# Two-layer diffusion trunk on one core: residual with tokens on partitions, down and output projections with weight rows moving

## The chip, the core and the metric

The kernel runs on one core of a Trainium2 chip. TensorE (PE in the profile) multiplies, VectorE (DVE), ScalarE (ACT) and GpSimd (POOL) work on SBUF, the on-chip memory with 128 partitions, and SyncE (SP) issues the transfers from HBM. A matmul holds a stationary operand of 128x128, whose load is a record of its own (PEld), and streams a moving operand of up to 512 columns through it into one of eight accumulator banks of 128 partitions by 512 floats (PSUM). The metric is the device time of one execution in microseconds (us), as the median of several runs; smaller is better.

## The reference, cut to what matters

There are two layers over 256 context and 256 latent tokens (one sequence of 512 here) of 1024 features. The mixing itself (attention, neighbourhood attention, delta rule, state space) does not change. What the change touches are the norms around each stage and the products before them:

```python
def rms_norm(x, g):
    xf = x.astype(jnp.float32)
    y = xf * lax.rsqrt(jnp.mean(xf * xf, axis=-1, keepdims=True) + RMS_EPS)
    return (y * g.astype(jnp.float32)).astype(x.dtype)

def modulate(x, g_pre, shift, scale):
    return rms_norm(x, g_pre) * (1.0 + scale) + shift

def half_ffn(v, shift, scale, gate, g_pre, g_post, w1, w3, w2):
    out = swiglu(modulate(v, g_pre, shift, scale), w1, w3, w2)   # (silu(h @ w1) * (h @ w3)) @ w2
    return v + 0.5 * gate * rms_norm(out, g_post)

# one layer, for the latent tokens h (the context hc has the same weights and its own modulation)
    h = half_ffn(h, ml[0], ml[1], ml[2], g[0], g[1], ffn1_w1[l], ffn1_w3[l], ffn1_w2[l])
    ul = modulate(h, g[2], ml[3], ml[4])
    y_lat, y_ctx = token_mixing(ul, uc, ...)                     # ends in [a, b, c, d] @ w_out
    h = h + ml[5] * rms_norm(y_lat, g[3])
    h = half_ffn(h, ml[6], ml[7], ml[8], g[4], g[5], ffn2_w1[l], ffn2_w3[l], ffn2_w2[l])
```

So a norm over the features of each token stands before and after each of three stages per layer. w1 and w3 are 1024x2816, w2 is 2816x1024, w_out is 1024x1024. In the last layer the context is not needed after the mixing, so its last FFN runs on 256 latent tokens. The nine modulation vectors of a layer come from `silu(c) @ w_mod`.

## The kernel before

**Arithmetic.** Each factor is kept as a high part, rounded to fp32r, and a low part, the rest. A product is three matmuls (`split_product`, lines 885 to 887): high by high, high by low, low by high.

**Layout.** Residual and activations have features on partitions: `xT` is 8 blocks of 128 features by 512 tokens. In every product of an FFN and of the output projection a 128x128 block of weights is stationary and 512 tokens move. One FFN has two parts. Each part has 11 "up" pieces (a block of w1 and of w3, 8 feature blocks each, 48 matmuls of 512 columns) into banks 0 to 3, a silu on ACT, a product on DVE and a split into `hh` and `hl`, and then 8 "down" pieces (1408 floats per partition, 33 matmuls of 512 columns), each of which gives one block of 128 output features in bank 4 or 7. The part's results are collected in `uT` by DVE. The last FFN already has weights moving in its down projection: `hh_last` and `hl_last` are stationary there, and `x_turn` (L1478) and `gate_rows` (L1487) bring residual and gain to that layout; its tail from L2066 on ACT and L2818 on DVE norms and adds token tiles of 128.

**Weights.** SP brings pieces of 2048 floats per partition (512 KB) into a ring of four slots, ACT rounds a piece to `wh` (L1617), DVE subtracts to get `wl` (`split_rest`, L2137) or, for the first piece of a stage, POOL does (`split_first`, L2874). `wh` and `wl` have two buffers (`wh_in`, `wl_in` for the input projection), so piece n waits for the products of piece n-2.

**Gaps.** Between two stages (five times: after the first FFN and after the output projection of each layer, and after the second FFN of layer 0) nothing can be multiplied until the norm of the result, the residual and the norm of the new residual are done. Before, with features on partitions, the sum over features goes through TensorE: DVE squares and adds blocks (`y_block`, L2240, L2243), PE adds over partitions (`token_sums`, L841), ACT takes the root (L1622), DVE the reciprocal (L2189), and PE broadcasts it (`spread`, L833). Then DVE scales (L2254) and adds (L2258, blocks 2 and 5 on POOL), ACT squares (L1657), and the same way leads through sums, root and spread to DVE L2218 and L2214, to the high parts on ACT and the low parts on DVE (L2230, L2225) and POOL. PE has three modulation products in each of these gaps (`mod_product`, L818; `GAP_MODS = 3`), which it does while it waits, with a small turn (L798) behind them. The first piece of the next stage then goes through feature blocks k = 0 to 7 as they come.

**Order.** All five engines have instruction streams written out by hand, which meet by semaphores. Within an engine nothing overtakes.

## Time and profile before

| | us |
|---|---|
| median of 3 runs | 2214.09 (2212.1 to 2214.68) |
| profiled execution | 2218.34 |
| its span, first to last instruction | 2216.5 |
| mean granted TensorE clock | 0.966 |

| engine | busy us | share of the span | instructions |
|---|---|---|---|
| PE | 2080.9 | 94% | 12805 |
| DVE | 1060.7 | 48% | 1570 |
| ACT | 788.0 | 36% | 1201 |
| POOL | 199.6 | 9% | 298 |

Busy time says how full an engine is over the whole. The chain that ended last says whose work sets the end at each moment. For this kernel the windows between two stages have to be read by themselves, since the average hides them: the stage before ends with its last product, and the next one runs evenly again with its second piece. Of HBM the transfers take 116 GB/s on average.

### The profile page before, as it was taken

To read this page: it belongs to the slowest core of one execution; us is meant where nothing else is said; L and a number is where in the kernel's file an instruction comes from. 1 tells how busy PE (TensorE), PEld (TensorE's weight loads), DVE (VectorE), ACT (ScalarE), POOL (GpSimd) and SP (SyncE) were. 2 spreads that over 40 slices of the span, in tenths; PEclk is the share of its full clock that TensorE was granted. 3 is DMA by queue.
4 is the path that set the end of the run, shared out by engine and by line. 5 is a ranking of instruction groups with operands and counts; after the bars stand their busy time and mean duration, and the time that the engine had idled before them with its cause. 6 is when DMAs were issued, how large, how long until landed. Compare 5 with 4: busy or idle time off the path is not lost.

```text
span 2216.5 us, 30333 instructions
## 1 busy us (share of the span) xinstructions
PE 2080.9 (94%) x12805; PEld 1700.1 (77%) x12805; DVE 1060.7 (48%) x1570; ACT 788.0 (36%) x1201; POOL 199.6 (9%) x298
## 2 busy tenths in 40 slices
PE   6999999899989998999999899999979987888998
PEld 4778888687846776888888688888859764687997
DVE  5233333566285576333334633333464548475554
ACT  3222222354335335221223522222344434344443
POOL 0000000100024421000000100000010022521000
PEclk8999999999999999999999899999988998899999
DMA  9554443423236433424423432432342311335653
GB/s 293 162 172 130 125 110 85 148 77 100 69 115 217 153 96 96 114 66 117 113 72 106 119 97 76 121 95 73 112 131 69 107 39 39 115 115 153 181 185 109
DMA packets 383752, 258.88 MB, mean 117 GB/s; under 512 B 21738, under 2 KB 379392, under 8 KB 383616
## 3 DMA queue, kind: packets, MB, share of 16 engines
q1 hardware_dynamic: 383616, 256.94, 39.5%
q8 instruction: 101, 1.65, 0.3%
q14 instruction: 35, 0.29, 0.0%
HBM read 255.86 MB, written 1.05 MB: 116 GB/s over the span
## 4 chain that ended last, share of the span: by engine, by line
PE 81%; DVE 12%; ACT 3%; issue 1%; SPq 1%; POOL 1%; DMA 0%; DVEq 0%; ACTq 0%; POOLq 0%
PE bank L885 23%; PE bank L886 23%; PE bank L887 23%; PE bank L818 2%; PE bank L1252 1%; DVE mlaw L2480 1%; DVE arena L2487 1%; DVE uT L2254 1%; PE bank L1390 1%; DVE small L2508 1%; DVE wl L2137 1%; PE bank L841 1%; PE bank L833 1%; ACT wh L1617 1%; PE bank L1361 1%
## 5 line engine op out<-in xcount | busy, mean ns | idle before, releaser
L885 PE MATMUL bank<-uh,wh 128*128 128x512 f32 (+1 forms) x1504 | 548.7, 365 | 11.1 <-DVE ul L2230 6.5
L887 PE MATMUL bank<-uh,wl 128*128 128x512 f32 (+1 forms) x1504 | 545.8, 363 | 0.0
L886 PE MATMUL bank<-ul,wh 128*128 128x512 f32 (+1 forms) x1504 | 545.8, 363 | 0.0
L2137 DVE TENSOR_TENSOR wl<-ring,wh 128x2048 fp32r<-128x2048 f32 (+1 forms) x150 | 311.7, 2078 | 175.6 <-ACT wh L1617 175.4
L1617 ACT ACTIVATE wh<-ring 128x2048 fp32r<-128x2048 f32 (+1 forms) x153 | 266.3, 1741 | 304.9 <-PE bank L887 293.0
L885 PEld LDWEIGHTS bank<-uh,wh 128*128 128x128 f32 x1504 | 286.1, 190 | 61.7 <-issue 12.0
L887 PEld LDWEIGHTS bank<-uh,wl 128*128 128x128 f32 x1504 | 285.9, 190 | 43.7
L886 PEld LDWEIGHTS bank<-ul,wh 128*128 128x128 f32 x1504 | 286.1, 190 | 43.0
L2276 DVE TENSOR_TENSOR arena<-arena,bank 128x512 f32<-128x512 f32 x66 | 45.4, 688 | 353.0 <-PE bank L887 353.0
L885 PE MATMUL bank<-hh,wh 128*128 128x512 f32 x528 | 205.5, 389 | 0.0
L887 PE MATMUL bank<-hh,wl 128*128 128x512 f32 x528 | 205.4, 389 | 0.0
L886 PE MATMUL bank<-hl,wh 128*128 128x512 f32 x528 | 205.4, 389 | 0.0
L1715 ACT ACTIVATE hh<-arena 128x512 fp32r<-128x512 f32 x66 | 41.8, 634 | 350.4 <-DVE arena L2276 350.4
L885 PE MATMUL bank<-uTh,wh_in 128*128 128x512 f32 (+2 forms) x320 | 123.9, 387 | 13.5 <-DVE wl_in L2137 5.9
L886 PE MATMUL bank<-ul_in,wh_in 128*128 128x512 f32 (+2 forms) x320 | 120.9, 378 | 0.0
L887 PE MATMUL bank<-uTh,wl_in 128*128 128x512 f32 (+2 forms) x320 | 120.8, 378 | 0.0
L885 PEld LDWEIGHTS bank<-hh,wh 128*128 128x128 f32 x528 | 99.1, 188 | 20.7
L887 PEld LDWEIGHTS bank<-hh,wl 128*128 128x128 f32 x528 | 99.1, 188 | 20.5
L886 PEld LDWEIGHTS bank<-hl,wh 128*128 128x128 f32 x528 | 99.1, 188 | 20.5
L1713 ACT ACTIVATE arena<-bank 128x512 f32<-128x512 f32 x66 | 39.5, 598 | 155.0 <-PE bank L887 155.0
L1772 ACT ACTIVATE arena<-bank 128x512 f32<-128x512 f32 (+5 forms) x64 | 30.5, 479 | 174.5 <-PE bank L887 174.3
L885 PEld LDWEIGHTS bank<-uTh,wh_in 128*128 128x128 f32 (+1 forms) x320 | 62.1, 194 | 31.6 <-issue 8.5
(349 smaller groups left out, 2840.2 us busy)
## 6 DMA issues: line engine op xcount, KB each, us to landing
ring<-in_ffn_w_dram SPq DMA_DIRECT2D x198, 512.0 KB, 5.2
ring<-in_w_mod_dram SPq DMA_DIRECT2D x134, 512.0 KB, 4.6
ring<-in_w_in_dram SPq DMA_DIRECT2D x40, 512.0 KB, 4.7
ring<-in_ffn_w_dram SPq DMA_DIRECT2D x48, 384.0 KB, 3.6
ring<-in_ffn_w_dram SPq DMA_DIRECT2D x48, 320.0 KB, 4.3
ring<-in_w_out_dram SPq DMA_DIRECT2D x16, 512.0 KB, 4.2
arena<-in_w_mod_dram SPq DMA_DIRECT2D x10, 512.0 KB, 9.1
ring<-in_w_in_dram SPq DMA_DIRECT2D x4, 544.0 KB, 5.8
```

Source lines behind the costliest of these rows:

```text
L818: product = pe.matmul(bank[at, 256:512], scT[:, own:own + 32], weights[:, k * 256:(k + 1) * 256], start=g == first and k < 4, stop=g == fi ...
L833: last = pe.matmul(bank[:, i * P:(i + 1) * P], cst[at, C_TILE + i:C_TILE + i + 1].to_broadcast([P - at.start, P]), inverse[at, :], start=T ...
L841: done = pe.matmul(bank[32 * i:32 * i + 32, 0:P], ones[:, 0:32], squares[:, i * P:(i + 1) * P], start=first, stop=last)
L885: pe.matmul(bank, w_hi, x_hi, start=first, stop=False)
L886: pe.matmul(bank, w_hi, x_lo, start=False, stop=False)
L887: return pe.matmul(bank, w_lo, x_hi, start=False, stop=last)
L1617: A(high[:, SPLIT[n] % 2, 0:floats], ring[:, n % RING, 0:floats], ACT.Copy).then_inc(wh_ready, 1)
L1713: A(silu_t[:, j % 2, t0:T], ps[2 * (j % 2)][:, t0:T], ACT.Silu).then_inc(silu_done, 1)
L1715: A(hh[:, j, t0:T], silu_t[:, j % 2, t0:T], ACT.Copy).then_inc(hh_ready, 1)
L1772: A(dst, src, ACT.Copy, scale=scale).then_inc(proj_copied, 1)
L2137: TT(low[:, b, 0:floats], at, high[:, b, 0:floats].bitcast(F32), ALU.subtract).then_inc(wl_ready, 1)
L2276: TT(ht, ht, ps[2 * (j % 2) + 1][:, t0:T], ALU.mult).then_inc(gated, 1)
```

## The change

The residual is kept with tokens on partitions: `x_rows`, four tiles of 128 tokens by two halves of 512 features. In down and output projections the activations are stationary, 128 tokens at a time, and the weight rows move in 512 columns, so that the eight banks hold the whole result (four token tiles by two halves). `ffn` of PE goes through pieces of one or two k-blocks (`DOWN_BLOCKS`), with 24 matmuls of 512 columns for each block; the last piece goes bank by bank. Part 0's result of the first five or four banks (`kept_over`) is copied to `uT` by ACT, the rest stays in its bank for part 1 to add to.

The norms are per-token scalars: ACT squares with an accumulating output (`y_stat`, `x_stat`) and takes roots, DVE has `read`, `update` and `scale` for each tile, POOL multiplies the kept banks by the gate's row (`gain_rows`). For this the gate times gain vector has to stand along the columns on all partitions: `spread_rows` makes it in chunks of 512 by four broadcast matmuls each, and ACT moves it (`move_rows`). The normed tiles are turned back to features on partitions by TensorE (`turn`, eight transposes for each tile), and scaled by gain and shift for each half of the tokens (256 columns). The first piece of a stage goes through them in two halves of 256 columns (`up_piece`, fresh). The three modulation products of a gap come after that piece (`gap_group`).

In the output projection a piece is four k-blocks by 512 columns (`out_piece`), and piece 0 (48 matmuls) stands before the turn of the scan's output, where 24 stood. Setup norms x before its 32 transposes. `x_turn` and `gate_rows` fall away.

The diff, cut to its core, goes through the plan of the pieces, then PE, ACT, DVE and POOL. Only its added lines stand here; what they take the place of are the functions printed above.

```diff
+    DOWN_BLOCKS = {True: (1, 2, 2, 2, 2, 1, 1), False: (1, 2, 2, 2, 2, 2)}
...
+def kept_over(q):
+    return 0 if q % 3 == 1 else 5 if q == 0 else 4
...
+    def turn(p, pos):
+        q, order = p - 1, pre_order(p)
+        half, t = pos // 2, order[pos]
+        pe.wait_ge(x_scaled, NT + tiles_before(q) + pos + 1)
+        if len(order) == NT:
+            pe.wait_ge(y_sq, 2 * tiles_before(q) + 4 * half + 4)
+            pe.wait_ge(y_read, 2 * tiles_before(q) + 4 * half + 4)
         for m in range(KC):
+            at = (m % 2) * HALF + (t % 2) * P
+            last = pe.transpose(turn_bank(p, half, m)[:, at:at + P],
+                                scaled_at(q, pos)[:, m // 4, (m % 4) * P:(m % 4 + 1) * P], ident)
+        last.then_inc(x_turned, 1)
...
+    def spread_rows(q, halves_of, banks):
+        pe.wait_ge(post_ready, q + 1)
+        chunks_of = [(h, i) for h in halves_of for i in range(2)]
+        for n, (h, i) in enumerate(chunks_of):
+            if n >= len(banks):
+                pe.wait_ge(rows_moved, rows_before(q) + n - len(banks) + 1)
+            for m in range(4):
+                last = pe.matmul(ps[banks[n % len(banks)]][:, m * P:(m + 1) * P],
+                                 gpost[:, q % 3, 4 * i + m, h:h + 1].to_broadcast([P, P]), ident,
+                                 start=True, stop=True)
+            last.then_inc(rows_spread, 1)
...
+                if k + count < HB:
+                    for at in range(count):
+                        pe.wait_ge(hl_ready, g0 + k + at + 1 + GATE_CREDIT)
+                        for b in (4, 5, 6, 7, 2, 3, 0, 1):
...
+                            last = product(n, k + at, at, b)
+                    last.then_inc(pieces_done, 1)
+                else:
+                    pe.wait_ge(hl_ready, g0 + HB + GATE_CREDIT)
+                    for b in range(8):
+                        for at in range(count):
+                            last = product(n, k + at, at, b)
+                        if b == 7:
+                            last.then_inc(pieces_done, 1)
+                        elif part or b < kept_over(q):
+                            last.then_inc(y_ended, 1)
...
+    def out_piece(l, j):
+        q = 3 * l + 1
+        order = order_of(q)
+        i, half = divmod(j, 2)
+        n = PIECES["out", l][j]
+        pe.wait_ge(wl_ready, SPLIT[n] + 1)
+        high, low = (wh_out[:, 0], wl_out[:, 0]) if j == 0 else (wh[:, SPLIT[n] % 2], wl[:, SPLIT[n] % 2])
+        for pos in range(len(order)):
+            ts = slice(order[pos] * P, (order[pos] + 1) * P)
+            for k in range(4):
+                if pos == 0:
+                    out_low(pe, l, 4 * half + k)
+                last = split_product(y_bank(q, 2 * pos + i)[:, :], (uh[:, 4 * half + k, ts], ul[:, 4 * half + k, ts]),
+                                     (high[:, k * 512:(k + 1) * 512], low[:, k * 512:(k + 1) * 512]),
+                                     half == 0 and k == 0, half == 1 and k == 3)
+            if half and pos < len(order) - 1:
+                last.then_inc(y_ended, 1)
+            if j == 1 and pos == 0:
+                spread_rows(q, halves(l, True), range(len(order)))
+        last.then_inc(pieces_done, 1)
...
+    def gap(q):
+        if len(order_of(q)) == NT:
+            y_stat(q, 0)
+            y_stat(q, 1)
+            x_stat(q + 1, 0)
+            y_stat(q, 2)
+            x_stat(q + 1, 1)
+            y_stat(q, 3)
+            x_stat(q + 1, 2)
+            x_stat(q + 1, 3)
...
+                round_piece(PIECES[f"up{part + 1}", l, f][0], 2048)
+                for b in range(kept_over(q)):
+                    act.wait_ge(y_ended, ended_before(q) + b + 1)
+                    A(uT[:, b, :], ps[b][:, :], ACT.Copy).then_inc(part_moved, 1)
...
+    def gap(q):
+        p, order, base, kept = q + 1, order_of(q), 2 * tiles_before(q), kept_over(q)
+        def read(b):
+            pos, i = divmod(b, 2)
+            if b < kept:
+                wait_ended(dve, q, b)
+                TT(uT[:, b, :], uT[:, b, :], ps[b][:, :], ALU.add).then_inc(y_read, 1)
...
+            dve.wait_ge(y_sq, base + b + 1)
+            if i == 0:
+                mean(Y_MEAN, Y_ACC, pos)
+            TT(gained_at(q, b), y_bank(q, b)[:, :], gate_rows[2 * (order[pos] // 2) + i], ALU.mult
+               ).then_inc(y_read, 1)
+        def update(pos):
+            dve.wait_ge(y_rooted, tiles_before(q) + pos + 1)
+            link(V.reciprocal(column(Y_INV, pos), column(Y_STD, pos)))
+            for b in (2 * pos, 2 * pos + 1):
+                if b < kept:
+                    dve.wait_ge(row_gained, moved_before(q) + b + 1)
                 else:
+                    dve.wait_ge(y_read, base + b + 1)
+                x = x_rows[:, order[pos], b % 2, :]
+                STT(x, gained_at(q, b), column(Y_INV, pos), x, ALU.mult, ALU.add).then_inc(x_updated, 1)
...
+        dve.wait_ge(rows_moved, rows_before(q) + len(order))
+        for b in range(3):
+            read(b)
+        update(0)
+        read(3)
+        update(1)
+        scale(p, 0)
+        if len(order) == NT:
+            read(4)
+            read(5)
+            update(2)
+            read(6)
+            scale(p, 1)
+            read(7)
+            update(3)
+            scale(p, 2)
+            first_made(p)
+        last_mean()
+        scale(p, len(order) - 1)
+        prenorm_blocks(p, len(order) == NT)
...
+    def gain_rows(q):
+        pool.wait_ge(rows_moved, rows_before(q) + len(order_of(q)))
+        for b in range(kept_over(q)):
+            pos, i = divmod(b, 2)
+            pool.wait_ge(y_read, 2 * tiles_before(q) + b + 1)
+            G.tensor_tensor(gained_at(q, b), uT[:, b, :], gate_rows[2 * (order_of(q)[pos] // 2) + i], ALU.mult
+                            ).then_inc(row_gained, 1)
...
+            gain_rows(3 * l - 1)
             split_first(PIECES["up0", l, 0][0], 2048)
```

The order on three places of the instruction streams follows; a name's trailing number is left out, `uTh` and `ul_in` are the high and low parts of the normed input, `cst` holds the identity.

PE, end of the first FFN of layer 0, before: the last block's sums of squares (L841), the third modulation product (L818), the broadcast (L833) and turn (L798), and the first products of the input projection.

```order
L841 MATMUL bank<-arena,cst 32x128 [waits x_squared]
L841 MATMUL bank<-arena,cst 32x128 x3
L818 MATMUL bank<-ring,scT 32x256 [waits weights_landed0]
L818 MATMUL bank<-ring,scT 32x256 x7
L833 MATMUL bank<-arena,cst 128x128 [waits inverse_ready]
L833 MATMUL bank<-arena,cst 128x128 x3
L798 MATMUL bank<-cst,mod_row 128x3x2 [waits row_copied]
L798 MATMUL bank<-cst,mod_row 128x3x2
L885 MATMUL bank<-uTh,wh_in 128x512 [waits ul_ready,wl_ready]
L886 MATMUL bank<-ul_in,wh_in 128x512
L887 MATMUL bank<-uTh,wl_in 128x512
L885 MATMUL bank<-uTh,wh_in 128x512
```

The same place in the changed kernel:

```order
L978 MATMUL bank<-wh,hl 128x512
L948 MATMUL bank<-cst,arena 128x128 [waits y_read,y_sq,x_scaled]
L948 MATMUL bank<-cst,arena 128x128 x7
L948 MATMUL bank<-cst,arena 128x128 [waits y_read,y_sq,x_scaled]
L948 MATMUL bank<-cst,arena 128x128 x7
L948 MATMUL bank<-cst,arena 128x128 [waits y_read,y_sq,x_scaled]
L948 MATMUL bank<-cst,arena 128x128 x7
L948 MATMUL bank<-cst,arena 128x128 [waits y_read,y_sq,x_scaled]
L948 MATMUL bank<-cst,arena 128x128 x7
L976 MATMUL bank<-uTh,wh 128x256 [waits low_ready,wl_ready]
L977 MATMUL bank<-ul_in,wh 128x256
L978 MATMUL bank<-uTh,wl 128x256
```

Four turned tiles stand where sums, modulation products and broadcast stood, and the products have 256 columns. The first piece's end in the changed kernel:

```order
L976 MATMUL bank<-uTh,wh 128x256
L977 MATMUL bank<-ul_in,wh 128x256
L978 MATMUL bank<-uTh,wl 128x256
L928 MATMUL bank<-ring,scT 32x256 [waits mod_copied,weights_landed2]
L928 MATMUL bank<-ring,scT 32x256 x7
L928 MATMUL bank<-ring,scT 32x256 [waits weights_landed3]
L928 MATMUL bank<-ring,scT 32x256 x7
L928 MATMUL bank<-ring,scT 32x256 [waits weights_landed0]
L928 MATMUL bank<-ring,scT 32x256 x7
L908 MATMUL bank<-cst,mod_row 128x3x2 [waits row_copied]
L908 MATMUL bank<-cst,mod_row 128x3x2
L976 MATMUL bank<-uTh,wh_in 128x512 [waits low_ready,wl_ready]
```

The modulation products and their turn have moved between the first piece and the second, which starts with L976 in 512 columns.

DVE at the same gap, before: the scaling of y by the broadcast bank (L2254) and the addition to the residual (L2258).

```order
L2189 RECIPROCAL arena<-arena 128x128 [waits rms_ready]
L2254 TENSOR_TENSOR uT<-uT,bank 128x512 [waits y_gained,inverse_spread]
L2254 TENSOR_TENSOR uT<-uT,bank 128x512 [waits y_gained]
L2258 TENSOR_TENSOR xT<-xT,uT 128x512 [waits y_scaled]
L2254 TENSOR_TENSOR uT<-uT,bank 128x512 [waits y_gained]
L2258 TENSOR_TENSOR xT<-xT,uT 128x512 [waits y_scaled]
L2254 TENSOR_TENSOR uT<-uT,bank 128x512 [waits y_gained] x2
L2258 TENSOR_TENSOR xT<-xT,uT 128x512 [waits y_scaled]
L2254 TENSOR_TENSOR uT<-uT,bank 128x512 [waits y_gained]
L2258 TENSOR_TENSOR xT<-xT,uT 128x512 [waits y_scaled]
L2254 TENSOR_TENSOR uT<-uT,bank 128x512 [waits y_gained] x2
L2258 TENSOR_TENSOR xT<-xT,uT 128x512 [waits y_scaled] x2
```

In the changed kernel, the last two tiles: L2389 scales a tile, L2410 reads a bank of the down projection, L2422 updates the residual, L2356 makes blocks of the next norm from the turned banks. The first two tiles stand ahead in the same way, with L2402 adding kept banks.

```order
L2388 RECIPROCAL stat<-stat 128x1 [waits x_rooted]
L2389 TENSOR_SCALAR arena<-xT,stat 128x1024 [waits dve_link]
L2410 TENSOR_TENSOR arena<-bank,arena 128x512 [waits y_sq]
L2415 RECIPROCAL stat<-stat 128x1 [waits y_rooted]
L2422 SCALAR_TENSOR_TENSOR xT<-arena,stat,xT 128x512 [waits y_read,dve_link]
L2422 SCALAR_TENSOR_TENSOR xT<-arena,stat,xT 128x512 [waits y_read]
L2388 RECIPROCAL stat<-stat 128x1 [waits x_rooted]
L2389 TENSOR_SCALAR arena<-xT,stat 128x1024 [waits dve_link]
L2356 TENSOR_SCALAR arena<-bank,gpre,modT 128x256 [waits x_turned] x4
L2393 TENSOR_SCALAR stat<-stat 128x1 [waits x_halved]
L2388 RECIPROCAL stat<-stat 128x1 [waits x_rooted]
L2389 TENSOR_SCALAR arena<-xT,stat 128x1024 [waits dve_link]
```

Each token tile goes through the whole of it on DVE, with one-column reciprocals (L2415, L2388) between the passes.

PE, end of the scan of layer 0, before: the last of the 24 early products, the turn of the scan's output (L1445), and the rest of the first pieces' blocks.

```order
L886 MATMUL bank<-ul,wh_out 128x512
L887 MATMUL bank<-uh,wl_out 128x512
L1445 MATMUL bank<-cst,arena 128x128 [waits scan_normed]
L1445 MATMUL bank<-cst,arena 128x128 x15
L885 MATMUL bank<-uh,wh_out 128x512 [waits ul_ready,y_copied,wl_ready]
L886 MATMUL bank<-ul,wh_out 128x512
L887 MATMUL bank<-uh,wl_out 128x512
L885 MATMUL bank<-uh,wh_out 128x512 [waits ul_ready]
```

In the changed kernel:

```order
L977 MATMUL bank<-wl_out,uh 128x512
L978 MATMUL bank<-wh_out,ul 128x512
L1591 MATMUL bank<-cst,arena 128x128 [waits scan_normed]
L1591 MATMUL bank<-cst,arena 128x128 x15
L976 MATMUL bank<-wh,uh 128x512 [waits ul_ready,wl_ready]
L977 MATMUL bank<-wl,uh 128x512
L978 MATMUL bank<-wh,ul 128x512
L976 MATMUL bank<-wh,uh 128x512 [waits ul_ready]
```

What follows the turn is no longer the rest of piece 0 but piece 1, which waits for its own low part (wl_ready); the gain rows (L964) stand behind its first tile.

## Rows read from the trace of the kernel before

**Rows 1.** The page's chain that ended last: shares of the span by engine.

```profile
PE 81%; DVE 12%; ACT 3%; issue 1%; SPq 1%; POOL 1%; DMA 0%; DVEq 0%; ACTq 0%; POOLq 0%
```

**Rows 2.** Windows: the five gaps, then an even stretch, a restart, 256 columns.

```profile
core 0: us, PE busy (x) PEld busy (x) DVE busy (x) ACT busy (x) POOL busy (x), PEclk, DMA share, GB/s
418.80:452.78 33.98, 23.64 (x198) 16.40 (x197) 25.81 (x45) 22.95 (x41) 10.58 (x7) 0.85 0.42 127
852.22:885.54 33.32, 23.95 (x197) 16.51 (x196) 25.21 (x45) 21.63 (x39) 5.91 (x4) 0.85 0.39 102
1233.84:1267.70 33.86, 24.57 (x198) 16.95 (x197) 25.21 (x45) 21.61 (x39) 5.91 (x4) 0.80 0.48 125
1615.99:1649.94 33.95, 20.30 (x198) 14.10 (x197) 25.37 (x45) 23.97 (x41) 10.54 (x7) 0.80 0.42 127
1997.20:2022.88 25.68, 16.64 (x150) 11.79 (x148) 17.77 (x39) 14.43 (x29) 4.29 (x5) 0.87 0.63 164
900.00:1000.00 100.00, 100.00 (x443) 82.81 (x442) 33.96 (x28) 26.29 (x27) 0.00 (x0) 1.00 0.28 79
439.39:442.51 3.12, 3.12 (x7) 2.45 (x8) 3.12 (x8) 2.71 (x7) 0.00 (x0) 0.50 0.26 38
2026.41:2036.00 9.59, 9.59 (x82) 9.59 (x81) 4.47 (x4) 2.99 (x4) 0.00 (x0) 1.00 0.56 148
```

**Rows 3.** Timeline of PE in the first gap: start, duration, line, form, count.

```profile
418.89 1.07 PE L818 MATMUL bank<-ring,scT 128*32 128x256 f32 x16
...
436.25 0.51 PE L798 MATMUL bank<-cst,mod_row 128*128 128x6 f32 x4
...
452.78 0.50 PE L885 MATMUL bank<-uTh,wh_in 128*128 128x512 f32 x1 [0.73 <-DVE wl_in L2137]
```

**Rows 4.** Timeline of ACT and DVE in the tail, one tile of the last norm.

```profile
2207.78 0.60 ACT L2066 ACTIVATE arena<-bank 128x512 f32<-128x512 f32 x1 [0.67 <-PE bank L887]
...
2208.57 0.30 ACT L2071 ACTIVATE std<-small 128x1 f32<-128x1 f32 x1
...
2208.51 0.69 DVE L2818 TENSOR_TENSOR xT<-bank,uT 128x512 f32<-128x512 f32 x1 [0.61 <-ACT arena L2066]
2209.11 0.15 DVE L2822 RECIPROCAL rst<-std 128x1 f32<-128x1 f32 x1
2209.30 1.41 DVE L2825 SCALAR_TENSOR_TENSOR xT<-xT,rst,uT 128x512 f32<-128x512 f32 x2
```

**Rows 5.** Groups of DVE by form: a scaling of 1024 columns in SBUF.

```profile
L2494 DVE TENSOR_SCALAR arena<-arena,cst 128x1024 f32<-128x1024 f32 x2 | 1.5, 744 | 0.0
```

**Rows 6.** Timeline of POOL and DVE in the gap after layer 1's output projection.

```profile
1993.69 4.63 POOL L2874 TENSOR_TENSOR wl<-ring,wh 128x2048 fp32r<-128x2048 f32 x1 [27.42 <-ACT wh L1617]
...
1994.98 3.63 DVE L2240 TENSOR_TENSOR arena<-uT 128x256 f32<-128x256 f32 x1
...
1999.43 0.43 DVE L2240 TENSOR_TENSOR arena<-uT 128x256 f32<-128x256 f32 x1
```

**Rows 7.** Timeline of PE in the last FFN: gate_rows and x_turn.

```profile
2060.78 1.95 PE L1487 MATMUL bank<-cst,gpost 128*128 128x128 f32 x16
...
2036.00 1.91 PE L1478 MATMUL bank<-cst,xT 128*128 128x128 f32 x16
```

**Rows 8.** Groups by form: rounding and splitting a piece of 2048.

```profile
L1617 ACT ACTIVATE wh<-ring 128x2048 fp32r<-128x2048 f32 x105 | 200.1, 1906 | 110.4 <-PE bank L887 98.5 <-DMA ring<-in_ffn_w_dram 11.9
...
L2137 DVE TENSOR_TENSOR wl<-ring,wh 128x2048 fp32r<-128x2048 f32 x102 | 233.8, 2292 | 149.8 <-ACT wh L1617 149.7
```

**Rows 9.** Timeline of PE and ACT at the start of a down projection (part 1).

```profile
358.95 0.39 PE L885 MATMUL bank<-hh,wh 128*128 128x512 f32 x1
...
359.88 0.63 ACT L1715 ACTIVATE hh<-arena 128x512 fp32r<-128x512 f32 x1 [5.56 <-DVE arena L2276]
...
361.93 1.37 ACT L1617 ACTIVATE wh<-ring 128x1408 fp32r<-128x1408 f32 x1
```

**Rows 10.** Timeline of PE and DVE at layer 0's output projection.

```profile
802.60 0.77 PE L885 MATMUL bank<-uh,wh_out 128*128 128x512 f32 x1 [3.38 <-DVE arena L2715]
...
811.46 1.97 PE L1445 MATMUL bank<-cst,arena 128*128 128x128 f32 x16 [0.75 <-DVE arena L2757]
...
816.41 2.29 DVE L2137 TENSOR_TENSOR wl<-ring,wh 128x2048 fp32r<-128x2048 f32 x1 [0.53 <-ACT wh L1617]
```

942 lines of the change are left out of this document (471 added, 471 removed).

## The prediction

> **What bounds the kernel now.** I read the chain that ended last first: 81% of it is PE, then DVE with 12% [rows 1]. A product of 512 columns follows the last one after 100.00/443 us = 0.226 us, or, by single starts of neighbouring rows, 0.2267, with PE busy throughout [rows 2]. So in the stages the number of columns sets the time, and this number stays: down and output projection have as many products as before. What can change is where PE waits. These places are the five gaps [rows 2]: from the last product to the second piece of the next stage 33.98, 33.32, 33.86, 33.95 and 25.68 us. In the first, modulation products start at once after the last product (418.89), 16 records in 1.07 us, a turn of 0.51 us stands at 436.25, and the second piece starts at 452.78 [rows 3]. All this work lies in the waiting. So the sum is: new gaps against old ones, plus all new PE work outside of them, plus new waits inside the stages. It is made on the profiled execution (2218.34 us, span 2216.5), which lies 4.3 us above the median of 2214.09. A change under 0.2% (4.4 us) is about what a measurement of this kernel can't tell from none.
>
> **Norms in the gap.** The unit prices come from the tail, where the same operations run on token tiles already [rows 4]: square with sum 0.79 us on ACT (2207.78 to 2208.57), root 0.30, read of a bank on DVE 0.69 (0.66 in a row), reciprocal of one column 0.15 (0.17 with its wait), update of 512 columns 1.41/2 = 0.70. Scaling 1024 columns costs 0.74 [rows 5], a block of 256 about 0.42 [rows 6], eight transposes 1.91/16 x 8 = 0.96, by starts 0.92 [rows 7].
>
> For an FFN with four kept banks, DVE has behind the start of `update(1)`: six updates 4.2, four scalings 3.0, four reads 2.6, six reciprocals 1.0, three means 0.45, four blocks 1.6 and a wait for a root 0.36, together 13.2 us without a pause. When does it start? POOL has the four gains, and then `split_first`. That split took 4.63 us, and the DVE operation with SBUF inputs that began inside it took 3.63 instead of 0.43 [rows 6]: it ended only with the split. In the changed order the split starts at -1.6 us (zero is the end of the last product), when the gains are through and the rounded piece is there, and lasts to +2.9. `update(1)` has two inputs in SBUF and stands still until then. 2.9 + 13.2 + 0.92 (the last turn) = 17.05 us to the first product.
>
> The Trainium skill, SBUF — State Buffer, "Who interferes with whom", says the same in general: VectorE and GpSimd share a port pair in SBUF, a VectorE instruction with two SBUF inputs and a GpSimd instruction exclude each other, and whoever is second waits for the whole of the first. By that rule, the trace agrees (3.63 against 0.43 us). Without such a rule the kept gaps would be 4 to 5 us shorter, which is the third rival below.
>
> With five kept banks (first gap) one more gain shifts the split and the end: 17.75. After layer 0's output projection nothing is kept and the split lies before the end. DVE has 17.6 us of such work (eight reads, eight updates, four scalings, eight reciprocals, five means, four blocks) from tile 0's end at -8.2 us: 10.4 with 1 us of square and root ahead, 0.92 for the turn and small waits give 11.9. Layer 1 has two tiles and a split that reaches to +1.1: 10.3. Then the first piece follows in 256 columns: 96 products by 0.117 us (82 in 9.59) = 11.2 us, 5.6 with latent tokens alone. After such a wait PE goes at clock 0.50: 7 products took 3.12 us [rows 2], so over 3.4 us some 1.6 us are lost. And the modulation products, hidden until now, stand between first and second piece: 3 x 1.04 + 0.5, and about 0.5 for the row's copy in between, 4.2 us [rows 3]. With 0.3 for the second piece's start:
>
> - after FFN 1, layer 0: 17.75 + 17.3 = 35.05 against 33.98, **+1.1**
> - after the output projection, layer 0: 11.9 + 17.3 = 29.2 against 33.32, **-4.1**
> - after FFN 2, layer 0: 17.05 + 17.3 = 34.35 against 33.86, **+0.5**
> - after FFN 1, layer 1: the first piece is halved, but the next one waits for its low part, which DVE splits behind the blocks, at 28.6; with the 4.2 us 32.8 against 33.95, **-1.1**
> - after the output projection, layer 1: 10.3 + 5.6 + 1.6 + 4.5 = 22.0 against 25.68, **-3.7**
>
> Together -7.3 us. The bound from below: if DVE had no backlog at the end, only the last tile's chain would stand in a gap, square 0.79, root 0.30, mean 0.15, read 0.69, reciprocal 0.15, update 1.41, then the same square, root, mean and reciprocal 1.4, scaling 0.74, turn 0.92, a block, its high and low part 1.2: 7.6 us in place of 17.75, 11.9, 17.05, 10.3. From above: each price as measured with gaps (reads 0.69, starts 0.05 later for 30 steps), +1.5 for each gap.
>
> **Gate rows.** `spread_rows` is the same operation as `gate_rows`: 8 matmuls, 1.95 us, by starts 1.70 to the next product [rows 7]. In three FFNs and layer 0's projection there are 16 of them, 3.4 us, and in the FFNs, where two banks serve four chunks, 0.35 for ACT to clear the first: 3 x 3.75 + 3.4. Layer 1's projection has 8: 1.7. The last FFN had 16 transposes (1.66) and 1.70 of gate rows, and now has 1.70. They stand between products that could run, so nothing hides them: 11.25 + 3.4 + 1.7 - 1.66 = **+14.7 us**.
>
> **Second down piece.** The first down piece was 33 products, 7.5 us, and is 24, 5.44 us. Its follower must be rounded behind the last `hh` and a table load: that rounding starts at 361.93, 2.98 us after the first down product at 358.95 [rows 9]. Of 2048 floats it takes 1.91, the split 2.29 [rows 8]: 7.2 us. Without the table load (part 0) 5.75. So PE, which until now had cover for that, waits 1.7 and 0.3, in three FFNs: **+6.0**. The later pieces have 10.9 us of products against 4.2, no wait. Copies of kept banks by ACT lie beside products of up pieces, no cost as long as up piece 0 of part 1 needs banks 0 to 3 only after them, which the bank-by-bank end gives 1.36 us each for.
>
> **Output projection.** In layer 0 the early products start at 802.60 and the turn stands at 811.46, after 0.75 us of waiting for DVE; 24 products fit before, up to 810.7 [rows 10]. Now 48 stand there: the turn comes 24 x 0.2267 = 5.4 us after the former end of the early ones at 810.7, so at 816.1, 4.7 later. The next piece's low part, split from 816.41 for 2.29 [rows 10], comes 4.7 later as well, at 823.4, and PE, done with the turn at 817.9, waits for it: until now it had the rest of piece 0, whose operands were there. From 823.4, 144 products take 32.6 us, to 856.1, with the start's wait 856.4, against 852.2: +4.2, and 1.6 for the slow clock after 5.6 us of idleness. Layer 1, without early products, +0.4 for one piece more waiting: **+6.2** together. Both sides: nothing, if rounding overtook, to +9.
>
> **The rest.** One more modulation turn (0.51 [rows 3]) and a start with the norm ahead of the transposes, where nothing hides it, 0.5: **+1.0**. The transfers keep their sum; at a DMA share of 0.28 in the even stretch [rows 2] they have room.
>
> Sum: -7.3 + 14.7 + 6.0 + 6.2 + 1.0 = **+20.6 us**, 2238.9 on the profiled execution, 2234.7 by the median; I take 2234.
>
> **Rivals.**
> 1. *The waits are longer than the clock forgives* (slower still). PE now stands idle for 10 to 17 us in each gap, where it had sums and modulation products in between. If the lost clock then lasts twice as long, 5 x 1.6 + 1.6 at the projection = +10 us: about 2244. For it: the old restart at 0.50 after just 2.6 us of waiting. Against: nothing shows a longer one.
> 2. *The norm is hidden beside the last piece* (faster). The last down piece ends bank by bank, 1.36 us each, and tiles 0 to 2 need about 4 us of DVE each. If squares and reads keep up, and the split on POOL comes before the updates, only the last tile's chain of 7.6 us remains: -10.1 - 4.3 - 9.4 - 9.4 (the wait for the low part goes as well) - 2.7 = -36, 2199. It decides on DVE's backlog at the last product: under 3 us it wins, with my 13.2 it does not. For it: 9.5 us between first and last bank.
> 3. *The port does not bite.* If updates run beside the split, or the split comes at another time, the three gaps after FFNs are 4 to 5 us shorter: -13.5, 2221. For it: at the first gap of before, readings of banks went at full speed beside a split.
>
> **How the numbers follow.** Forecast 0.62 at 2234 (own range 2225 to 2242), rival 1 0.10, rival 3 0.12, rival 2 0.16 in all its degrees, most of which would stop halfway near 2215. The range of 8 in 10 reaches from rival 3 with some of rival 2, 2216, to rival 1 with the upper bounds, 2248. Faster by over 0.2%: rival 2 but for a little, 0.15. Within 0.2%: its halfway cases and a part of rival 3, 0.10. Slower: 0.75.
>
> **What would show it.** In the profile after: first products of a stage 17 to 18 us after the last one behind FFNs and 10 to 12 behind output projections; DVE without pause in between; an update of 3 us or more beside POOL's split; L928 groups on PE behind the first piece at full price; L964 with 3.4 to 3.8 us; PE waiting for wl, released by DVE, at the second down piece; the same at the second output piece, some 5.6 us. It is wrong if DVE is idle in the gaps (then the chain of waits counts, not the sum of work), if products with weights moving have another pitch than 0.2267, or if ACT's squares, and not DVE, hold up the tiles.

## The result, and the profile after

| | before | changed |
|---|---|---|
| median | 2213.78 us | 2251.92 us |
| range of the runs | 2212.1 to 2214.68 | 2249.02 to 2253.09 |
| profiled execution | 2218.34 | 2249.02 |
| its span | 2216.5 | 2247.2 |
| mean granted clock | 0.966 | 0.962 |

The changed kernel is slower by 1.62% (ratio 1.0162, 95% interval 1.0150 to 1.0175), 38 us between the medians. A second set of runs gave 2251.89 us and a ratio of 1.0170 (1.0156 to 1.0184). The 2213.78 us are the median of four executions; the 2214.09 us that the prediction starts from were that of three of them. The prediction had the sign right, and with 2234 us and 2216 to 2248 it missed the size: the time lies 4 us above its range.

The chain of the changed kernel reads nearly like the one before [rows 1]; as shares of so long a span it hides all that follows:

```profile
PE 80%; DVE 12%; ACT 3%; issue 2%; SPq 1%; DMA 1%; POOL 0%; DVEq 0%; ACTq 0%; POOLq 0%
```

The difference is found stage by stage. The table is worked out from the starts of TensorE's products in both timelines: a stage goes from its first product to the end of its last one (a product's pitch behind its start), "first piece" from its first product to the second piece's first one, "wait" from the last product of one stage to the first of the next.

| stage | before | changed | difference |
|---|---|---|---|
| start, to the first product | 37.2 | 36.9 | -0.4 |
| FFN 1, layer 0 | 381.6 | 388.5 | +6.9 |
| wait | 20.6 | 18.4 | -2.2 |
| first piece | 13.4 | 17.4 | +4.0 |
| rest of the input projection and mixing, layer 0 | 349.8 | 349.9 | 0.0 |
| output projection, layer 0 | 49.6 | 59.8 | +10.1 |
| wait, first piece | 20.0 + 13.3 | 12.4 + 16.3 | -4.6 |
| FFN 2, layer 0, behind its first piece | 348.3 | 354.7 | +6.4 |
| wait, first piece | 20.5 + 13.3 | 17.4 + 16.6 | +0.1 |
| FFN 1, layer 1, behind its first piece | 348.3 | 354.7 | +6.4 |
| wait | 20.6 | 17.4 | -3.2 |
| input projection, layer 1 | 158.5 | 167.5 | +9.1 |
| mixing, layer 1 | 169.8 | 166.5 | -3.3 |
| output projection, layer 1 | 32.3 | 36.2 | +3.9 |
| wait, first piece | 16.4 + 9.3 | 12.1 + 11.0 | -2.6 |
| last FFN, behind its first piece, to the end | 193.6 | 193.7 | 0.0 |
| sum | 2216.5 | 2247.2 | +30.7 |

The waits themselves, by the windows of the changed kernel (the same places as the first five of [rows 2], but here only up to the first product; then 3.44 us behind the first of them):

```profile
core 0: us, PE busy (x) PEld busy (x) DVE busy (x) ACT busy (x) POOL busy (x), PEclk, DMA share, GB/s
425.37:443.76 18.39, 6.81 (x34) 5.62 (x33) 16.44 (x29) 10.26 (x31) 7.06 (x4) 0.66 0.18 57
870.76:883.17 12.41, 6.81 (x33) 5.61 (x33) 11.70 (x27) 8.75 (x26) 1.33 (x2) 0.66 0.08 19
1254.15:1271.55 17.40, 7.69 (x34) 6.33 (x33) 16.66 (x30) 10.11 (x31) 4.46 (x3) 0.58 0.22 61
1642.83:1660.23 17.40, 7.69 (x34) 6.33 (x33) 16.66 (x30) 10.11 (x31) 4.45 (x3) 0.60 0.19 60
2030.47:2042.52 12.05, 3.83 (x18) 3.31 (x17) 9.06 (x17) 6.16 (x17) 2.13 (x2) 0.70 0.33 88
443.76:447.20 3.44, 3.44 (x18) 3.44 (x17) 3.44 (x8) 1.65 (x5) 0.93 (x2) 0.50 0.00 0
```

DVE is busy 16.66 of 17.40 us behind an FFN. Every one of the waits is shorter than before. What is longer stands around them: work that had been hidden in the wait, and waits inside the stages. The largest of these is seen on PE and ACT in layer 1's input projection (timeline of PE, then of ACT):

```profile
1685.05 2.80 PE L928 MATMUL bank<-ring,scT 128*32 128x256 f32 x48
1694.91 1.02 PE L908 MATMUL bank<-cst,mod_row 128*128 128x6 f32 x4 [7.06 <-ACT mod_row L1715]
```

```profile
1691.70 1.91 ACT L1741 ACTIVATE wh_in<-ring 128x2048 fp32r<-128x2048 f32 x1 [22.30 <-DMA ring<-in_w_in_dram]
1693.51 1.07 ACT L1927 ACTIVATE arena<-bank 128x512 f32<-128x512 f32 x2
1694.47 0.39 ACT L1715 ACTIVATE mod_row<-bank 128x256 f32<-128x256 f32 x1
```

The three modulation products end at 1687.8, and then TensorE stands for 7.06 us in front of their turn, for a row of 0.39 us that ACT takes out only behind a rounding, which itself had waited 22.30 us for a transfer. That transfer was late because SP could not issue it. The waits of SP's queue from 1645 to 1700 us, and then the queue's timeline from 1686 us:

```profile
SPq L720 <- PE bank L928: 39.3, 1, 39.3
```

```profile
1686.18 1.93 SPq L720 DMA_DIRECT2D ring<-in_w_in_dram  x2
```

SP stood for 39.3 us in front of the third weight piece, until the first of the three modulation products had been done and its slot of the ring was free. (A full piece is 1 MB, two transfers of 512 KB, not one as said above.) The prediction had 4.2 us for this group and no wait.

### The profile page after: what moved, and what is told of

Its sections match the earlier page's. It is cut to its first block, busy times and chain, and to the rows that moved or that the text cites. A ratio compares the mean times of both kernels' runs of the same rounds, so it can differ in the third digit from the quotient of the medians.

```text
span 2247.2 us, 30025 instructions
## 1 busy us (share of the span) xinstructions
PE 2083.9 (93%) x12625; PEld 1716.9 (76%) x12625; DVE 1004.7 (45%) x1497; ACT 783.1 (35%) x1244; POOL 203.2 (9%) x311
## 4 chain that ended last, share of the span: by engine, by line
PE 80%; DVE 12%; ACT 3%; issue 2%; SPq 1%; DMA 1%; POOL 0%; DVEq 0%; ACTq 0%; POOLq 0%
PE bank L976 23%; PE bank L977 23%; PE bank L978 23%; PE bank L928 2%; DVE xT L2422 2%; PE bank L1398 1%; DVE wl L2288 1%; DVE mlaw L2660 1%; ACT wh L1741 1%; DVE arena L2667 1%; DVE small L2688 1%; PE bank L1536 1%; PE bank L964 1%; SPq L720 0%; PE bank L1301 0%
## 5 line engine op out<-in xcount | busy, mean ns | idle before, releaser
L976 PE MATMUL bank<-uh,wh 128*128 128x512 f32 (+1 forms) x1440 | 522.3, 363 | 4.8 <-DVE ul L2365 2.7
L977 PE MATMUL bank<-ul,wh 128*128 128x512 f32 (+1 forms) x1440 | 519.5, 361 | 0.0
L978 PE MATMUL bank<-uh,wl 128*128 128x512 f32 (+1 forms) x1440 | 519.0, 360 | 0.0
L2288 DVE TENSOR_TENSOR wl<-ring,wh 128x2048 fp32r<-128x2048 f32 x139 | 310.1, 2231 | 423.2 <-ACT wh L1741 423.2
L976 PEld LDWEIGHTS bank<-uh,wh 128*128 128x128 f32 x1440 | 275.0, 191 | 50.2 <-issue 8.0
L976 PE MATMUL bank<-wh,hh 128*128 128x512 f32 x528 | 206.1, 390 | 6.4 <-DVE wl L2288 5.0
L977 PE MATMUL bank<-wl,hh 128*128 128x512 f32 x528 | 205.4, 389 | 0.0
L978 PE MATMUL bank<-wh,hl 128*128 128x512 f32 x528 | 205.4, 389 | 0.0
L976 PEld LDWEIGHTS bank<-wh,hh 128*128 128x128 f32 x528 | 99.1, 188 | 28.9 <-DVE wl L2288 7.3
L976 PE MATMUL bank<-uTh,wh_in 128*128 128x512 f32 (+2 forms) x288 | 113.0, 392 | 6.4 <-DVE wl_in L2288 6.4
L978 PEld LDWEIGHTS bank<-wh,hl 128*128 128x128 f32 x528 | 99.1, 188 | 20.7
L977 PEld LDWEIGHTS bank<-wl,hh 128*128 128x128 f32 x528 | 99.1, 188 | 20.4
L3050 POOL TENSOR_TENSOR arena<-uT,mlaw 128x512 f32<-128x512 f32 x8 | 10.3, 1296 | 737.0 <-DVE uT L2402 736.9
```

The lines of the kernel that those rows point to most:

```text
L976: pe.matmul(bank, w_hi, x_hi, start=first, stop=False)
L977: pe.matmul(bank, w_hi, x_lo, start=False, stop=False)
L978: return pe.matmul(bank, w_lo, x_hi, start=False, stop=last)
L2288: TT(low[:, b, 0:floats], at, high[:, b, 0:floats].bitcast(F32), ALU.subtract).then_inc(wl_ready, 1)
```

## The experiments

Each edit is one to the changed kernel, unless it is said to stand on top of others, and medians are to be read against its 2251.9.

**Where the port counts: the split put first.** Three gaps behind FFNs, POOL's order:

```diff
-                gain_rows(3 * l)
                 split_first(PIECES["in", l][0], 2048)
+                gain_rows(3 * l)
```

> Only change to the changed kernel: on POOL, the split of the next stage's first weight piece stands before the multiplications of the kept banks by the gate's row instead of behind them (three gaps, after FFNs). Theory (the split holds the port that DVE's updates need, and DVE has a backlog): the update of 4.86 us at 429.48 in the changed kernel falls to 1.4, the split now lies at about -9 to -4 us before the last product, beside reads that take a bank, and each of the three gaps is 2 to 4 us shorter, 2240 to 2246 in all against 2251.9. Rival (the updates wait for what POOL delivers, not for the port): now POOL's products come 4.5 us later, updates wait for them, and the gaps stay as long or grow by up to 2 us each, 2250 to 2258.

Measured: 2255.64 us, and the waits were 19.2, 17.6 and 17.6 instead of 18.4, 17.4 and 17.4. The theory's outcome did not come, the rival's did. (Of the 3.7 us the three waits are 1.3; in this profile layer 1's mixing was 3.4 us longer too.) The timelines of the third wait show why: POOL and DVE of the changed kernel first, then of this one.

```profile
1252.74 4.54 POOL L3041 TENSOR_TENSOR wl<-ring,wh 128x2048 fp32r<-128x2048 f32 x1
...
1248.68 2.14 DVE L2422 SCALAR_TENSOR_TENSOR xT<-arena,stat,xT 128x512 f32<-128x512 f32 x2
1250.74 0.68 DVE L2402 TENSOR_TENSOR uT<-uT,bank 128x512 f32<-128x512 f32 x1
1253.02 0.16 DVE L2415 RECIPROCAL stat<-stat 128x1 f32<-128x1 f32 x1 [1.61 <-ACT stat L1751]
1253.22 5.27 DVE L2422 SCALAR_TENSOR_TENSOR xT<-arena,stat,xT 128x512 f32<-128x512 f32 x2
```

```profile
1249.38 4.24 POOL L3050 TENSOR_TENSOR arena<-uT,mlaw 128x512 f32<-128x512 f32 x3
...
1250.79 3.38 DVE L2422 SCALAR_TENSOR_TENSOR xT<-arena,stat,xT 128x512 f32<-128x512 f32 x2 [2.88 <-POOL arena L3050]
1254.09 0.67 DVE L2402 TENSOR_TENSOR uT<-uT,bank 128x512 f32<-128x512 f32 x1
1256.37 0.16 DVE L2415 RECIPROCAL stat<-stat 128x1 f32<-128x1 f32 x1 [1.60 <-ACT stat L1751]
1256.57 1.41 DVE L2422 SCALAR_TENSOR_TENSOR xT<-arena,stat,xT 128x512 f32<-128x512 f32 x2
```

In the changed kernel the second pair of updates takes 5.27 us and ends 1.2 us behind POOL's split (which ends at 1257.28): the port that the two engines share bites, as in [rows 6]. With the split ahead this pair takes 1.41. But the first pair now waits 2.88 us for POOL's gains and runs beside the next ones in 3.38 (2.14 in the changed kernel), so that the second pair ends 4.6 us behind the last product (1253.41) where it ended 4.3 behind it (1254.15). This moved the price and left the question open, hence the next but three.

**Modulation products back in the wait.** In all five gaps the group goes behind the first turned tile, in a bank already read (with two tiles ahead of them), and its turn behind the second:

```diff
             def prenorm(p):
+                if not four:
+                    products(1)
+                    mod_turn(first, bank)
                 for pos in range(len(pre_order(p))):
+                    if four and pos == 2:
+                        mod_turn(first, bank)
+                        pe.wait_ge(mod_copied, first + GAP_MODS)
                     turn(p, pos)
+                    if four and pos == 0:
+                        products(6)
```

> Only change to the changed kernel: the three modulation products of each of the five gaps, and their turn, go back into the waiting of TensorE (behind the first turned tile, in a bank that has been read; after layer 1's output projection ahead of it), instead of behind the first piece of the next stage. Theory (they cost their full price behind the first piece, 3.75 us in four gaps and 11 us in layer 1's first gap with its 7 us wait for ACT, and nothing in the wait): 4 x 3.7 + 11 less 3.3 us that a later stage gave back = 20 to 26 us faster, 2226 to 2232. Rival (their rows' copies on ACT and the restart of the clock lengthen the wait by what is saved): less than 8 us, 2244 or more.

Measured: 2226.14 us, 25.8 less. The first products of the next stage come as early as before (waits of 18.4, 12.4, 16.9, 17.3 and 12.4 us), although three products stand in each:

```profile
1262.43 4.27 PE L931 MATMUL bank<-ring,scT 128*32 128x256 f32 x48
1267.57 0.51 PE L911 MATMUL bank<-cst,mod_row 128*128 128x6 f32 x4
```

They take 4.27 us here, at a granted clock of 0.64, where the same group took 2.80 at 1.00 in the changed kernel (at 1685.05), and cost nothing. Layer 1's input projection went from 167.5 to 154.0 us, and no wait stands between its second and its third piece. The theory holds, at the upper end.

**Two k-blocks in the first down piece.**

```diff
-    DOWN_BLOCKS = {True: (1, 2, 2, 2, 2, 1, 1), False: (1, 2, 2, 2, 2, 2)}
+    DOWN_BLOCKS = {True: (2, 1, 2, 2, 2, 1, 1), False: (2, 1, 2, 2, 2, 2)}
```

> Only change to the changed kernel: the first two down pieces have 2 and 1 k-blocks instead of 1 and 2. Theory (the second piece's rounding and split can't be done in the 5.44 us of a one-block piece): the waits of 1.65 us at the second down piece of part 1 and the short ones of part 0 go, 5 to 6 us faster, 2246 to 2247. Rival (the wait is only moved to the third piece, whose buffer is the first one's): no change, 2250 to 2253.

Measured: 2248.39 us (2244.56 to 2251.14), 3.5 less by medians. In the changed kernel TensorE has this in part 1 of each FFN:

```profile
370.83 0.50 PE L976 MATMUL bank<-wh,hh 128*128 128x512 f32 x1 [1.65 <-DVE wl L2288]
```

In the timeline of this kernel no such wait is left at any of the six places, and the three FFNs are 2.0, 2.4 and 2.4 us shorter, 6.8 together. So the wait went and was not moved. That the medians show half of it is not explained by any run: the four executions stand in two groups, 2244.6 and 2245.7, 2251.0 and 2251.1, and the profiled one is the fastest of them although its mixing of layer 1 was long (172.1 us, see below).

**Half of the first output piece behind the turn.**

```diff
                 if early_out(l):
-                    out_piece(l, 0)
+                    out_piece(l, 0, range(len(order_of(3 * l + 1)) // 2))
                 pe.wait_ge(sem("scan_normed"), outputs_before(l, NT) // 2)
...
+                out_piece(l, 0, range(len(order_of(q)) // 2, len(order_of(q))))
```

> Only change to the changed kernel: of the first output piece, only the products of half of the token tiles stand before the turn of the scan's output, the other half behind it, in both layers. Theory (all of it ahead of the turn delays the turn and leaves TensorE nothing to do while the second piece's low part is made, 5.33 and 5.13 us): both waits go but for up to 1 us, and the slow clock behind them, so 9 to 12 us faster, 2240 to 2243. Rival (the wait is fed by ACT's order and stays behind the turn wherever the products are): 2 us or less, 2250 or more.

Measured: 2245.28 us, 6.6 less. In layer 0 the projection took 52.5 us instead of 59.8, and the wait shown here for the changed kernel is gone:

```profile
831.92 0.79 PE L976 MATMUL bank<-wh,uh 128*128 128x512 f32 x1 [5.33 <-DVE wl L2288]
```

In layer 1 it took 36.8 instead of 36.2. There the early products lie in a wait for the scan's output: the kernel before stands 4.38 us at the turn, the changed one 0.57, this one 3.32. So they are free ahead of the turn, and half of them behind it take away the wait of 5.13 us and bring 2.7 us back at the turn; with the slow clock behind that, nothing is won. The theory is right for one layer and wrong for the other.

**The split on DVE.** POOL's split is left out in the three gaps, and DVE does it where it was idle:

```diff
                 for b in range(3):
                     read(b)
+                    if b == 0 and q % 3 != 1:
+                        split_rest((PIECES["in", q // 3] if q % 3 == 0 else PIECES["up0", q // 3 + 1, 0])[0], 2048)
                 update(0)
```

> Only change to the changed kernel: in the three gaps behind FFNs the first weight piece of the next stage is split by DVE, right behind the first kept bank's addition, instead of by POOL behind the gains. It is the clean form of the question that the split put ahead of the gains left open, since the gains on POOL are now not delayed. Theory (the update stands still for 3.5 us because POOL's split has the port, and what follows it on DVE is a backlog without pause): the update pair of 4.86 to 5.27 us falls to 1.4, DVE pays 2.3 us in a stretch where it is idle, and each of the three gaps becomes 2 to 4 us shorter: from 18.4, 17.4, 17.4 to about 14.5, 13.6, 13.6; 2240 to 2246 in all. Rival (the gaps are bound by a chain through ACT and the last banks): the update gets shorter, DVE then waits, and the gaps stay within 1 us, 2249 to 2254.

Measured: 2248.85 us; the waits are 17.0, 15.4 and 15.4 us, 1.4, 2.0 and 2.0 shorter. DVE at the third one:

```profile
1247.72 2.28 DVE L2288 TENSOR_TENSOR wl<-ring,wh 128x2048 fp32r<-128x2048 f32 x1
1249.92 1.28 DVE L2402 TENSOR_TENSOR uT<-uT,bank 128x512 f32<-128x512 f32 x2
1252.20 0.17 DVE L2415 RECIPROCAL stat<-stat 128x1 f32<-128x1 f32 x1 [1.01 <-ACT stat L1751]
1252.40 2.47 DVE L2422 SCALAR_TENSOR_TENSOR xT<-arena,stat,xT 128x512 f32<-128x512 f32 x2
1254.80 0.68 DVE L2402 TENSOR_TENSOR uT<-uT,bank 128x512 f32<-128x512 f32 x1
1257.08 0.16 DVE L2415 RECIPROCAL stat<-stat 128x1 f32<-128x1 f32 x1 [1.60 <-ACT stat L1751]
1257.28 1.41 DVE L2422 SCALAR_TENSOR_TENSOR xT<-arena,stat,xT 128x512 f32<-128x512 f32 x2
```

The pair took 1.41 instead of 5.27, 3.9 us less, and 2.0 of them arrive at TensorE. The rest is the price of the edit: DVE's split of 2.28 us stands ahead of the reads, so that `read(3)` begins 1.6 us before the last product's end (1256.36), where it began 3.4 before it (1254.15), and the pair begins 0.9 us behind that end instead of 0.9 before it. The wait of 1.6 us for ACT's square and root stands in front of the pair in both kernels. From the end of the pair on DVE does the same passes in both, without a pause down to the last tile's root, and all of them 2.0 us earlier. So the theory's mechanism holds and the rival's does not, since DVE does not wait behind the pair; the gain is at the lower end or below, because the split was not free on DVE. What the lock alone costs lies between the 2.0 us measured and the 3.9 us of the pair, and no run here separates them.

**Rows, a quarter.**

```diff
-                    for m in range(4):
+                    for m in range(1):
                         last = pe.matmul(ps[banks[n % len(banks)]][:, m * P:(m + 1) * P],
```

> Only change to the changed kernel: of the four broadcast matmuls of each chunk of the gate rows only the first is done, in all norms behind FFNs and projections (three quarters of the gain are left at old values, so the result is another). Theory (they stand between products that could run, nothing hides them): 12 of 16 matmuls at 0.2125 us go in four places, 6 of 8 in two, 4 x 2.55 + 2 x 1.3 = 12.8 us less, 2238 to 2241. Rival (TensorE would wait there for weights anyway): less than 4 us.

Measured: 2244.30 us, 7.6 less, where 12.8 were expected. TensorE at the rows of FFN 2 of layer 0, in the changed kernel (the next product starts at 947.00) and with a quarter (next product at 941.43):

```profile
943.11 4.14 PE L964 MATMUL bank<-cst,gpost 128*128 128x128 f32 x32
```

```profile
938.61 0.61 PE L964 MATMUL bank<-cst,gpost 128*128 128x128 f32 x4
940.70 0.97 PE L964 MATMUL bank<-cst,gpost 128*128 128x128 f32 x4 [1.48 <-ACT mlaw L1842]
```

The stay is 3.89 us and falls only to 2.82: with two banks for four chunks, ACT's copies set a floor under the matmuls (the wait of 1.48). Layer 0's projection, with a bank for each chunk, became 3.1 us shorter; layer 1's did not, since the wait for its third piece grew (2.38 us against 2.10) and the projection took 36.7 us against 36.2. So the rows are not hidden, which was the question, but 7.6 and not 12.8 us are to be had from cheaper matmuls.

**Three and five edits together.** The group in the wait, the two-block first piece, and half of the output piece in layer 0 only:

```diff
+                    out_piece(l, 0, range(0, 2))
...
+                if len(order_of(q)) == NT:
+                    out_piece(l, 0, range(2, NT))
```

> The changed kernel with three edits together: modulation products back in the waits, two k-blocks in the first down piece, half of the first output piece behind the turn in layer 0 only. If their gains (25.8, 3.5 by medians or 6 by the trace, 6.6) add, 2213 to 2217; if the modulation products and the two-block piece give to each other's waits, above 2219.

Measured: 2214.37 us, against 2214.54 for the kernel before in the same runs (ratio 0.9996, 0.9984 to 1.0008), 37.5 less than the changed kernel, where the single gains by medians sum to 35.9. The gains add. With the split on DVE and, in `out_proj` of ACT,

```diff
                     round_piece(PIECES["out", l][j], 2048)
-                    if j == 1:
+                    if j == 2:
                         move_rows(q, halves(l, True), range(len(order_of(q))))
```

> As the kernel with three edits, and with DVE's split of the first piece, and with ACT's copies of the output projection's gate rows behind the rounding of the third piece (in layer 1 TensorE waited 2.1 us for that piece, which was rounded behind the copies). By the port theory three gaps are 3 to 4 us shorter and the wait of 2.1 us goes: 11 to 14 us below the kernel with three edits, 2200 to 2205, which would be faster than the kernel before. By the rival (chain through ACT) 2 us below it, 2211 to 2215.

Measured: **2198.64 us** (2197.27 to 2199.9), ratio to the kernel before 0.9925 (0.9908 to 0.9941): faster than both, by 0.75% than the kernel before. Its waits up to the first product are 16.8, 12.4, 15.3, 15.4 and 12.6 us, with the modulation products inside. The time lies below the range of the port theory, but not for its reason: against the profile with three edits the three waits behind FFNs are 1.7, 1.8 and 1.4 us shorter and not 3 to 4, the projection of layer 1 is 1.7 shorter, and the rest of the 14.8 us between the two spans is above all 3.2 in layer 1's input projection and 4.2 in its mixing, at a granted clock of 0.94 instead of 0.90. Why that clock was higher no run tells. Against the profile of the kernel before, 18.4 us shorter, the mixing of layer 1 counts for 4.3, but layer 0's input projection and mixing are 3.8 longer, so the gain does not rest on them. The window of the third wait:

```profile
1238.48:1253.82 15.34, 10.26 (x86) 6.77 (x85) 13.33 (x30) 11.62 (x35) 1.36 (x2) 0.78 0.51 132
```

**ACT's order or the ring.**

```diff
+                    if n == 2 and first_of(l, UNITS[0][4]) != 0:
+                        gap_group(l, 0)
                     if (n == 0 or j != UNITS[n - 1][1]) and j + 1 < len(IN_PIECES):
                         round_piece(PIECES["in", l][j + 1], KC * IN_WIDTH[j + 1], wh_in)
...
-                    if n == (1 if first_of(l, UNITS[0][4]) == 0 else 3):
+                    if n == 1 and first_of(l, UNITS[0][4]) == 0:
                         gap_group(l, 0)
```

> Only change to the changed kernel, in layer 1's input projection: ACT takes the modulation row out (and the column) before it rounds the third weight piece, not behind it. In the changed kernel TensorE waits 7.06 us at L908 for that row. Theory of the ring: the row was late because ACT stood 22 us in front of a rounding whose piece was still in flight; the piece was late because its slot of the four-slot ring held a modulation piece that TensorE now uses only behind units 2 and 3. Then this edit takes the wait at L908 away, but TensorE waits at the next piece for the same landing instead: the second half of the stage starts within 1 us of where it did, 2250 to 2253. Rival (ACT's order alone): the wait of 7 us goes and nothing takes its place, 2244 to 2246.

Measured: 2252.52 us, no change. The turn now comes at once, and then TensorE waits for the landing all the same:

```profile
1683.41 2.80 PE L928 MATMUL bank<-ring,scT 128*32 128x256 f32 x48
1686.71 0.61 PE L908 MATMUL bank<-cst,mod_row 128*128 128x6 f32 x4 [0.50 <-ACT mod_row L1715]
1694.83 0.79 PE L976 MATMUL bank<-uTh,wh_in 128*128 128x512 f32 x1 [7.50 <-DVE wl_in L2290]
```

The theory of the ring holds. A modulation piece that TensorE has not used keeps its slot of four, the weight piece behind it on SP's queue can't start (SP waits 39.2 us for TensorE here, 39.3 in the changed kernel), and the price of moving three products is a transfer, a rounding and a split in a row: 7.5 us. With the products back in the wait this was gone as well.

**The scaling on ACT.** On top of the five edits:

```diff
+                if p and pos < len(pre_order(p)) - 1:
+                    V.reciprocal(column(X_INV, pos), column(X_STD, pos)).then_inc(x_inverted, 1)
+                    return
...
                     y_stat(q, 2)
+                    x_scale(q + 1, 0)
                     x_stat(q + 1, 1)
                     y_stat(q, 3)
+                    x_scale(q + 1, 1)
                     x_stat(q + 1, 2)
+                    x_scale(q + 1, 2)
```

> The kernel with five edits (2198.6), and ACT instead of DVE multiplies the token tiles by their inverse root (L2389), all but the last tile of each gap: three passes of 0.75 us less on DVE in four gaps, one in the fifth, and passes of about 1.05 us more on ACT. Theory (in the gap DVE works off a backlog without pause, ACT has room): each of the four gaps becomes 2.0 to 2.3 us shorter, the fifth up to 0.7: from 16.75, 12.4, 15.34, 15.38, 12.64 to about 14.6, 10.3, 13.2, 13.2, 12.2; 2189 to 2192. Rival (the chain through ACT's squares and roots sets the pace, or will with 3 us more on it): gaps as long or up to 3 us longer, 2198 to 2210.

Measured: 2207.93 us, 9.3 more than with five edits; the waits are 17.6, 13.5, 16.8, 16.7 and 13.7, together 5.7 us longer. (In this profile the mixing of layer 1 took 172.1 us, 6.6 more; how much of the medians' difference beyond the waits that is can't be told.) The theory falls. The third wait's window:

```profile
1239.98:1256.80 16.82, 10.03 (x86) 6.64 (x85) 11.34 (x27) 14.77 (x38) 1.35 (x2) 0.80 0.46 120
```

DVE went from 13.33 to 11.34 us, ACT from 11.62 to 14.77, and the wait grew by 1.5: squares and roots of the next tile stand behind the scaling on ACT, and DVE, which had no pause there with five edits, now waits 1.35 us for ACT's square. So once the port is free the two engines alternate tile by tile, and in this order ACT has no time to take the passes.

**The changed kernel again.**

> The changed kernel once more, to see how far one profiled execution can stand from another of the same program. Theory: the profile of the changed kernel missed 7 us of the 38 us between the medians because the mixing stage of layer 1 takes one of several lengths in each execution, by short dips of the granted clock behind waits of 2 us: 166.5, 169.7 or 172.1 us so far, and layer 0's 202.5 or 206.5. Then the stages outside the mixing repeat within 0.5 us, and all of the difference to the first profile lies in the mixing. Rival: the difference is spread over the stages. Median 2249 to 2253 in either case.

Measured: 2251.89 us, profiled execution with a span of 2250.2, 3.0 us above the first. Layer 1's mixing took 169.69 us instead of 166.46, layer 0's 202.53 as before, and the five waits between stages are the same within 0.1 us. The theory's half microsecond was too narrow for the other stages, though: the first FFN took 0.7 us less, the last one 1.1 more behind its first piece (its wait for the third up piece was 3.4 instead of 2.1 us), and these and the first pieces nearly cancel. So by the mixing alone one profile can stand 3 us from another. Windows of layer 1's mixing in four profiles: the kernel before, the changed one, two blocks first, five edits.

```profile
1795.06:1964.86 169.80, 138.71 (x1416) 105.47 (x1415) 109.93 (x262) 65.99 (x159) 65.26 (x124) 0.90 0.24 69
```

```profile
1827.77:1994.23 166.46, 134.51 (x1415) 101.51 (x1415) 110.12 (x262) 65.99 (x159) 64.76 (x124) 0.93 0.24 71
```

```profile
1818.15:1990.24 172.09, 140.23 (x1415) 107.60 (x1415) 110.54 (x262) 66.00 (x159) 64.87 (x124) 0.88 0.24 69
```

```profile
1787.62:1953.12 165.50, 131.92 (x1416) 101.32 (x1415) 109.94 (x262) 66.03 (x159) 64.85 (x124) 0.94 0.24 71
```

The instructions are the same, and the length goes with the granted clock: 165.5 us at 0.94, 166.5 at 0.93, 169.8 at 0.90, 172.1 at 0.88.

## Why the prediction was wrong in size

Of the 17.9 us between 2234 and 2251.92, 10.1 lie in the sum, 7.2 in the step from the profile to the median (below), and 0.7 is the rounding from 2234.7. By its own steps, on the profiled executions, where it expected +20.6 us and +30.7 came:

| step | predicted | measured |
|---|---|---|
| gap after FFN 1, layer 0 | +1.1 | +1.8 |
| gap after the projection, layer 0 | -4.1 | -4.6 |
| gap after FFN 2, layer 0 | +0.5 | +0.1 |
| gap after FFN 1, layer 1, with the input projection | -1.1 | +5.9 |
| gap after the projection, layer 1 | -3.7 | -2.6 |
| three FFNs: gate rows, second down piece, one more turn | +17.8 | +19.7 |
| both output projections with their rows | +11.3 | +14.0 |
| start | +0.5 | -0.4 |
| last FFN without its transposes | -1.7 | 0.0 |
| mixing, layer 1 | 0 | -3.3 |

**The norms.** The first products were expected 17.75, 11.9, 17.05 and 10.3 us behind the last ones and came after 18.4, 12.4, 17.4 and 12.1. The prices from the tail [rows 4, 5] repeat: updates 1.41 for two, scaling 0.75, reads 0.69. Two values were off. A block of 256 columns with gain and shift took 0.54 us out of a bank (0.42 by [rows 6]); the same operation out of SBUF, at the start of the program, took 0.41. And the last turn took 1.62 us from its start to the first product, at a granted clock of 0.50, in four of the five waits, where 0.92 had been taken from full clock. Behind layer 1's projection the end was another one: the two turns stood together (3.68 us), DVE waited 2.33 for them, and the first product came with DVE's low part, 2.71 us behind the turns:

```profile
2036.13 3.68 PE L948 MATMUL bank<-cst,uT 128*128 128x128 f32 x16 [5.50 <-DVE uT L2389]
2042.52 0.55 PE L976 MATMUL bank<-uh,wh 128*128 128x256 f32 x1 [2.71 <-DVE ul L2365]
```

The bound from below was added up as 7.6 us, where its terms give 7.7. The lock was there, 5.27 for the pair. That without it the gap would be 4 to 5 us shorter is not borne out: the pair itself would be 3.9 shorter, and the run with the split on DVE brought 2.0, with the split's own time charged against it. Of the Trainium skill, SBUF — State Buffer, "Who interferes with whom", the runs agree with the rule that a VectorE instruction with two SBUF inputs and a GpSimd instruction that reads SBUF exclude each other (the pair ends 1.2 us behind POOL's split).

**The step that failed** is the modulation group in layer 1: "the next one waits for its low part ... at 28.6; with the 4.2 us 32.8". It priced the group by its own instructions and left out what holds the ring. The slot of the third piece was free only when the first modulation product was done, its transfer was issued at 1686.2, the piece landed at 1691.7, and its user waited: 7.06 us, with the group 11.0 in place of 4.2. What else stands in this row is clock and nearly cancels: the second and third pieces were 3.4 us longer than before, with 5.65 us at 0.50 behind the wait for the low part and 4.85 behind the wait for the row, and the same instructions behind the third piece were 3.1 us shorter than before (0.93 against 0.90). The same happened a second time, smaller, in the last FFN, where SP waits 18.0 us for a modulation product, the third up piece comes 2.12 us late, and this eats the gain of the removed transposes; with the products back in the wait, this wait too is gone.

**The FFNs.** Rows and second piece are as predicted: 3.89 (3.75), and 1.65 (1.7) and 0.30 (0.3) for the two parts. Not seen was a wait of 1.17 us in layer 0's first FFN, where the down projection, which now uses all eight banks, must have the last modulation column copied out (released by ACT, L1729).

**The projections.** Layer 0 came as worked out: the wait is 5.33 us (5.6), the whole +10.1 (+9.2 with rows and clock). Layer 1 was read wrongly ("without early products"): it has early products before and after the change, and they are free. Its +3.9 are, nearly, 1.7 of rows and 2.1 for the third piece, which ACT rounded behind the copies of the rows. The prediction placed the copies beside other work and did not ask what stands behind them on ACT; moving them behind that rounding was part of the five edits, and the wait of 2.1 us went.

**From profile to median.** The sum gave a difference and the prediction laid it on the median before, as if both profiles stood equally far from their medians. The profile before lies 4.3 us above the 2214.09 us and the one after 2.9 below its median: 7.2 of the 17.9 us by which the time was missed. Part of it is probably the mixing of layer 1 (3.3 us between these two; the second profile of the changed kernel, with 169.7 us there, lies on its median). The rest is open: the changed kernel's usual executions have a clock of 0.960, 20 of 34 of those before 0.967 to 0.970 (the others 0.962 to 0.966), and no run here tells in which stage the unprofiled ones lose it. With the modulation products back in the waits it was 0.966 again.

**The rivals.** At the five restarts the clock's loss did not last twice as long: behind waits of 18.4, 12.4, 17.4, 17.4 and 12.1 us TensorE ran 4.4, 1.9, 2.6, 3.1 and 3.1 us at 0.50, as against 3.12 before [rows 2]. The loss that did come lies behind the new waits inside layer 1's input projection. The last tile's chain alone (7.6 us) was never near. The port bites. So none of the rivals came; the missing one was "the modulation products hold the ring".

## What to carry to other kernels

When work that loads weights is moved later, count the slots that its pieces hold, for the price is a transfer with all that stands behind it and not the work itself. Work that needs no result of the wait belongs into the wait, if a bank is free for it, even where it runs at a lower clock. And when an engine looks like the bound of an alternating chain, take time off it in one run before moving load to its partner: what was taken off DVE here came back as waiting for ACT. And when load is moved to find out what a lock costs, subtract what the load costs in its new place.

## What the runs showed of the hardware

A stage with waits of up to 5.8 us for TensorE, of the same instructions, ran in 165.5 to 172.1 us in different executions, at granted clocks of 0.94 to 0.88. Such a stage should be left out when two profiles are compared. A pair of DVE updates beside POOL's multiplications of 512 columns took 2.14 to 3.38 us instead of 1.41, so that short POOL operations cost DVE time as well, not only the long split. It goes the other way too: with the split on DVE, the POOL multiplication that ran beside it took 3.22 us instead of 1.29. The new waits of 3.72 and 7.06 us inside a stage were followed by 5.65 and 4.85 us at a granted clock of 0.50.
